# First head's loads issued ahead of the last chunk's third pair of modulation loads, its low keys and biases one step sooner

## The reference, cut to what matters

```python
m_lat = adaln(c, w_mod[l], b_mod[l])                 # silu(c) @ w_mod + b_mod: six vectors of 2048, for c and c_ctx
h = modulate(rms_norm(ys, norm_mix[l]), m_lat[0], m_lat[1])
q, k, v, u = mixer_proj(h, w_in[l])                  # h @ w_in, 2048 x 4096
att = neighbourhood_attention(q, k, v, cache_k[:, l], cache_v[:, l], rpb[l])
mix = jnp.concatenate([att, pool_mixer(u, w_pool[l], pool_scale[l])], axis=-1) @ w_out[l]
ys = ys + m_lat[2][:, None] * mix
...
s_lat = q . k (window of 12 x 32 keys) * scale + bias   # bias from rpb, -1e30 outside the window
s_ctx = q . k_ctx (512 cached keys) * scale
p = softmax(concat(s_lat, s_ctx)); o = p @ (v, v_ctx)
```

## Time and profile before

| | |
|---|---|
| three runs | 3972.54 us (3972.15 to 3976.68) |
| the profiled execution | 3971.88 us, its span 3970.1 us |
| mean granted TensorE clock | 0.975 |
| PE busy over the span | 95% |
| PE / DVE / ACT / POOL busy, 1000 to 1200 us | 183.2 / 117.2 / 101.6 / 95.7 us |
| input projection ends | about 1064.5 us |
| attention | about 1065.7 to 1630 us |

### The profile page before, as it was taken

One profiled execution on the slowest core, in us unless ns is written; L12 is line 12 of the kernel. 1 busy time (PEld: TensorE's weight loads), 2 busy tenths in 40 slices (PEclk: granted clock), 3 DMA queues, 4 the chain that ended last, 5 costly groups with the idle time before them and its releaser, 6 DMA issues. The chain is left out here.

```text
span 3970.1 us, 63525 instructions
## 1 busy us (share of the span) xinstructions
PE 3764.5 (95%) x22936; PEld 3367.7 (85%) x22936; DVE 2455.5 (62%) x4637; ACT 1774.2 (45%) x2654; POOL 472.3 (12%) x517
## 2 busy tenths in 40 slices
PE   8999999999989999999987899999999999999992
PEld 4799999999988888888876788888888888888981
DVE  4745555555566666332225677777777777777774
ACT  3611111111367776311104666666666666665653
POOL 0000000000264644010101000000000000000000
PEclk9999999999999999999998899999999999999996
DMA  9434434433654645645317587888788778888886
GB/s 378 146 129 138 137 124 137 137 130 131 187 168 137 203 144 173 258 144 215 139 40 298 186 259 259 266 264 262 255 275 259 254 261 264 262 263 265 264 251 249
DMA packets 556531, 825.31 MB, mean 208 GB/s; under 512 B 24320, under 2 KB 426144, under 8 KB 544672
## 3 DMA queue, kind: packets, MB, share of 16 engines
q1 hardware_dynamic: 532384, 702.27, 53.4%
q0 software_dynamic: 24064, 121.93, 9.4%
HBM read 717.18 MB, written 108.00 MB: 208 GB/s over the span
## 5 line engine op out<-in xcount | busy, mean ns | idle before, releaser
L2159 DVE TENSOR_TENSOR e_wlo<-e_raw,e_whi 128x1024 fp32r<-128x1024 f32 x768 | 905.2, 1219 | 327.2 <-ACT e_whi L2078 323.9
L2296 PE MATMUL ps<-e_xs,e_whi 128*128 128x320 f32 x4096 | 1054.8, 344 | 10.0 <-DVE e_xs L2173 6.9
L2296 PE MATMUL ps<-e_xs,e_wlo 128*128 128x160 f32 x4096 | 934.9, 238 | 0.0
L2078 ACT ACTIVATE e_whi<-e_raw 128x1024 fp32r<-128x1024 f32 x768 | 766.0, 1049 | 284.8 <-DMA e_raw<-in_w_down 106.4
L2296 PEld LDWEIGHTS ps<-e_xs,e_wlo 128*128 128x128 f32 x4096 | 770.3, 191 | 0.7
L2296 PEld LDWEIGHTS ps<-e_xs,e_whi 128*128 128x128 f32 x4096 | 752.8, 188 | 14.4 <-issue 7.3
L2314 PE MATMUL ps<-e_whi,e_h 128*128 128x512 f32 x1024 | 403.1, 394 | 0.9 <-DVE e_h L2199 0.9
L531 PE MATMUL ps<-hhi,p_whi 128*128 128x428 f32 (+1 forms) x1536 | 381.8, 357 | 8.4 <-DVE p_wlo L463 8.4
L481 DVE SCALAR_TENSOR_TENSOR p_acc<-p_modraw,cT,p_acc 128x256 f32<-128x256 f32 x960 | 386.6, 478 | 0.3 <-DMA p_modraw<-in_w_mod 0.3
L531 PE MATMUL ps<-hlo,p_whi 128*128 128x428 f32 (+1 forms) x1536 | 382.4, 357 | 0.0
L531 PE MATMUL ps<-hhi,p_wlo 128*128 128x428 f32 (+1 forms) x1536 | 380.3, 356 | 0.0
(11 more groups left out here) (252 smaller groups left out, 5359.0 us busy)
## 6 DMA issues: line engine op xcount, KB each, us to landing
e_raw<-in_w_gate SPq DMA_DIRECT2D x64, 2048.0 KB, 7.9
e_raw<-in_w_up SPq DMA_DIRECT2D x64, 2048.0 KB, 7.8
e_raw<-in_w_down SPq DMA_DIRECT2D x64, 2048.0 KB, 8.0
p_modraw<-in_w_mod SPq DMA_DIRECT2D x128, 512.0 KB, 3.5
m_raw<-in_w_mod SPq DMA_DIRECT2D x16, 2048.0 KB, 13.3
p_raw<-in_w_in SPq DMA_DIRECT2D x64, 512.0 KB, 4.7
o_raw<-in_w_out SPq DMA_DIRECT2D x16, 2048.0 KB, 9.0
projT<-p_out_st POOLq DMA_DIRECT2D x30, 640.0 KB, 3.8
```

Source lines behind the costliest of these rows:

```text
L2078: nc.scalar.activation(piece(whi, c, q), piece(raw, c, q), ACT.Copy).then_inc(w_hi_made, 1)
L2159: nc.vector.tensor_tensor(piece(wlo, c, q), piece(raw, c, q), piece(whi, c, q).bitcast(F32), ALU.subtract).then_inc(w_lo_made, 1)
L2296: last = nc.tensor.matmul(bank[:, 0:cols], w[:, s, at:at + P], xs[:, k, 0:cols], start=(k == 0 and w is whi), stop=(k == KD - 1 and w is whi))
```

## The change

SP's loop now covers chunks 0 to 14, and chunk 15 is written out behind it. In chunk 15 `first_loads` comes behind the load of the third w_in quarter, ahead of the two w_mod pieces of that quarter, so ahead of the fourth w_in quarter too; it still waits for the stores of chunk 14 and for one used quarter. POOL makes the low keys once two quarters are used (three before), head 0's biases once three are, head 1's once four are. DVE makes the high keys behind the sums of the third quarter (q = 2) and no longer behind those of the fourth; low queries stay behind those of the fourth. To have the tiles free at these times, `kll` and `q8`, `prT`, `st` and `pscn` change rows, and `pu`, `inv` and `pd` go to a fixed offset in HIGH.

```diff
@@ sync
-            with sp.Fori(0, NCH) as n:
+
+            def load_chunk(n, head_after=None):
                 for q in range(NQ):
                     sp.wait_ge(w_lo_made, n * NQ + (q + 1))
                     sp.dma_start(raw[:, q % RING], quarter(w_in, q, n * CW)).then_inc(w_loaded[q % RING], 16)
+                    if q == head_after:
+                        sp.wait_ge(stored, 2 * LASTC * 16 + FIRST)
+                        sp.wait_ge(piece_used, quarters_used(1))
+                        first_loads()
                     for i in range(2):
                         m, part = q // 2, 2 * (q % 2) + i
                         sp.wait_ge(mod_step, n * (8 * QSTEPS) + (2 * q + i + 1) * QSTEPS)
                         sp.dma_start(modraw[:, i], quarter(w_mod, part, n * (2 * CW) + (MB0 * P + m * CW))
                                      ).then_inc(mod_in[i], 16)
-            sp.wait_ge(stored, 2 * LASTC * 16 + FIRST)
-            sp.wait_ge(piece_used, quarters_used(1))
-            first_loads()
+
+            with sp.Fori(0, LASTC) as n:
+                load_chunk(n)
+            load_chunk(LASTC, 2)
@@ gpsimd
+            pool.wait_ge(piece_used, quarters_used(2))
+            low_keys()
             pool.wait_ge(piece_used, quarters_used(3))
-            low_keys()
-            biases()
+            biases(0)
             pool.wait_ge(piece_used, quarters_used(4))
+            biases(1)
             pool.wait_ge(mod_turned, 2 * NCH + RING)
@@ vector
-                    if q == NQ - 1 and not following:
+                    if q == NQ - 2 and not following:
                         dve.wait_ge(piece_used, quarters_used(2))
                         high_keys()
+                    if q == NQ - 1 and not following:
                         low_queries()
@@ attention
-    mask, kraw, vc, kx, khh, q8, bias, prT, pairs, athi, pllo, st, pscn = row_of(
+    mask, kraw, vc, kx, khh, kll, bias, pairs, athi, pllo = row_of(
         LOW, ...
-    brow, qraw, vT, qst, vL, kll, atlo, plhi, wpn, pu, inv, pd = row_of(
+    brow, qraw, vT, qst, vL, q8, atlo, plhi, wpn, prT, st, pscn = row_of(
         HIGH, ...
+    pu, inv, pd = row_of(HIGH + 59 * 1024, ("pu", [P, PW], F32), ("inv", [P, TOK], F32), ("pd", [P, TOK], F32))
...
-        def biases():
+        def biases(h):
             pool.wait_ge(mask_in, 16)
-            make_bias(0, 0, True)
-            make_bias(0, 1, True)
+            make_bias(0, h, True)
```

More of the change, by code:

```diff
@@ L667, in attention @@
         ("a_mean", [P, 2, TOK], F32), ("pc", [P, 2, PW], F32))
-    mask, kraw, vc, kx, khh, q8, bias, prT, pairs, athi, pllo, st, pscn = row_of(
+    mask, kraw, vc, kx, khh, kll, bias, pairs, athi, pllo = row_of(
         LOW, ("mask", [P, 6, NKL], F32), ("kraw", [P, KCOL], F32), ("vc", [P, PAST // P, P], F32), ("kx", [P, CTX], F32),
-        ("khh", [P, 2, KCOL], F32R), ("q8", [P, TOK], F32),
-        ("bias", [P, 2, 6, NKL], F32),
-        ("prT", [P, 2, 1024], F32), ("a_pairs", [P, W, P], F32), ("athi", [P, TOK], F32R), ("a_pllo", [P, TOK], F32R),
-        ("a_st", [P, 4, 8], F32), ("a_pscn", [P, 1], F32))
-    brow, qraw, vT, qst, vL, kll, atlo, plhi, wpn, pu, inv, pd = row_of(
[L675 to L678, removed]
+        ("khh", [P, 2, KCOL], F32R), ("kll", [P, 2, KCOL], F32R), ("bias", [P, 2, 6, NKL], F32),
+        ("a_pairs", [P, W, P], F32), ("athi", [P, TOK], F32R), ("a_pllo", [P, TOK], F32R))
+    brow, qraw, vT, qst, vL, q8, atlo, plhi, wpn, prT, st, pscn = row_of(
+        HIGH, ("brow", [P, 2, 16 * 48], F32), ("qraw", [P, TOK], F32), ("vT", [P, TOK], F32),
+        ("qst", [P, 2, TOK], F32R), ("vL", [P, 4, KC * ROWS], F32), ("q8", [P, TOK], F32),
+        ("atlo", [P, TOK], F32R), ("a_plhi", [P, TOK], F32R), ("a_wpn", [P, 2, P], F32), ("prT", [P, 2, 1024], F32),
+        ("a_st", [P, 4, 8], F32), ("a_pscn", [P, 1], F32))
+    pu, inv, pd = row_of(HIGH + 59 * 1024, ("pu", [P, PW], F32), ("inv", [P, TOK], F32), ("pd", [P, TOK], F32))
     BATCH_AT = {1: 4, 12: 0, 14: 1, 17: 2, 19: 3}
```

## The result

The changed kernel takes 3979.52 us as the median of 20 runs (3971.47 to 3987.77); the kernel before, in 20 runs on the same chip, 3973.67 us (3964.17 to 3980.6). The medians differ by 5.9 us; the ratio is given as 1.0016 with a 95% interval of 1.0009 to 1.0023, so 6.4 us more with 3.6 to 9.1. That is within the 0.2% of "no change", and in the range of 3966 to 3982, at its slow end. The profiled execution took 3978.77 us, span 3977.0 us, mean granted clock 0.975.

A forecast was written before the change was run, and what follows sets the result against it. TensorE, busy 95% of the span, was taken as the bound. Terms 13.2 - 1.3 + 1.6 - 5.7 - 6.1 = +1.7 us on 3971.88 gave 3973.6, stated as a 3974.0 median; 8-in-10 range 3966 to 3982.

The forecast's parts named there:

- one turn each: Seam before attention: the last quarter's 16 sums alternate with POOL's instructions and end at 1076.0; this forecast had 0.50.
- The queue: SyncE, last chunk: head loads start 23.9 us sooner, w_in quarter 3 lands at 1045.9, costing PE nothing before 1048.2.
- POOL beside the sums: Seam before attention: late sums make PE wait at L540, first transpose at 1078.9 instead of 1065.69, +13.2 us.
- V copy: Start of attention: PE's 1.30 us wait for the V copy on ACT goes, -1.3 us.
- Clock at the start: Start of attention: PE leaves a long wait at low clock, +1.6 us net of the replaced stretch at 1074.
- Second head's wait: Second head: PE's 3.62 us wait for POOL's low keys goes with 2.1 us of clock, -5.7 us.
- The stall at L1104: First pair: PE's 4.18 us stall shrinks to 1.5 us, -2.7, and 3.4 us of clock goes, -6.1 us together.
- a rival: No exclusion for L481: sums end at 1061.8, total 3969.3, down to 3965.5 us; shared full queues might lessen gains; chance 0.13.
- The starved rival: Last sums and L1104: DVE gets no turn while POOL runs on, 3974.0 + 8.0 = 3982.0 us; chance 0.17.
- the 6.76 us row: L1104 beside POOL's run once took 6.76 us, outlasting several instructions; cited as evidence for DVE getting no turn.

The follow-up runs named there:

- version 2: Changed kernel, but POOL holds the first pair's biases until the last modulation sum, high keys staying early; median 3968.75 us, ratio 0.999 to the kernel before.
- 4: Kernel before plus twelve two-input POOL additions beside the sums of quarter 2 in the last chunk; one run, 3974.1 us.
- 3: Changed kernel with the first pair's twelve biases filled by memsets instead of computed; one run, 3964.09 us.
- 5: Kernel before plus 27 POOL memsets starting beside the sums of quarter 2 in the last chunk; one run, 3978.16 us.
- 1: Changed kernel with DVE's high keys back behind the last quarter's sums; median 3966.44 us, ratio 0.9995 to the kernel before.
- version 9: Kernel before with pauses between POOL's bias additions alone, low-key subtractions still end to end; 3955.27 us, ratio 0.9952.
- version 11: Changed kernel with pauses between POOL's bias additions alone; 3960.82 us, ratio 0.9969 to the kernel before.

## Why the prediction was right, and where its terms were off

The verdict, the sign and the range held, and the mechanism that I put first, one turn each between POOL and the sums, is what happened. Two terms were off, by -4.8 and +8.8 us, and it is partly luck that they cancelled as far as they did: with the first alone corrected the sum would have been below the kernel before. Term by term:

**The queue.** Quarter 3 of w_in reached ACT at +36.3, forecast +38.1. It cost PE nothing, as forecast. kx, 10.5 us from issue to landing (11.1 in the earlier trace rows), landed at 1038.5, that is +32.1 where I took +32.7; the three loads of 512 KB behind it then took 4.15 us, 379 GB/s, where I had taken 283 from the earlier trace rows. Two readings were rounded down, 4.26 us to 4.2 and 0.77 to 0.7; neither moves the sum. From the view of DMA issues, 1020 to 1068:

```profile
kx<-projT SPq DMA_DIRECT2D x1, 128.0 KB, 10.5
```

**POOL beside the sums, +13.2.** It measured +8.4; PE waited 7.08 us where I had said 11 to 13. One turn each was right: a median of 1230 ns a sum; versions 2 and 4 show the same price, 3 and 5 that memsets on POOL don't ask it. Too large were the landing and the keys behind it (high keys end at +45.6, not +47.6: 2.0 us), the sums (18.2 us behind the keys, not 20.6: 2.4) and the restart behind them (2.5 us, not 2.9: 0.4), which makes the 4.8. The Trainium skill (SBUF — State Buffer, "Who interferes with whom") has the second instruction to issue blocked for the whole of the first; the stream of sums agrees with it (1.23 us against 0.48 alone), the lone `atlo` of the first pair does not, since it outlasts up to ten of POOL's instructions.

**V copy, -1.3**: right (waits of 2.0 us in this stretch before, 0.7 after). **Clock at the start, +1.6**: low by about one. From the first transpose to the first `Kx` copy PE's stretch is 1.2 us longer in spite of the 1.3 won, so 2.5. The granted clock there, in windows (PEclk is third from the end; against 0.57 over 4 us in the earlier trace rows with 1.00 around it):

```profile
1072.60:1076.00 3.40, 3.29 (x13) 2.99 (x14) 0.63 (x2) 0.60 (x1) 3.10 (x5) 0.50 0.69 152
1076.00:1080.00 4.00, 2.89 (x13) 2.12 (x12) 2.30 (x8) 2.31 (x3) 0.14 (x1) 0.77 1.02 234
1080.00:1084.00 4.00, 2.67 (x9) 2.37 (x10) 0.77 (x2) 2.74 (x6) 0.00 (x0) 0.65 1.01 240
```

**Second head's wait, -5.7**: right in the profile, no wait at 1107.03 and the clock full over what follows:

```profile
1107.00:1111.30 4.30, 4.30 (x34) 4.03 (x34) 2.10 (x8) 3.26 (x7) 2.58 (x2) 1.00 1.04 224
```

But this wait is a difference of two chains and moves by itself: in versions 1, 2 and 9 it is 1.6 us, with no repair of it, and 4.0 in the kernel before with all pauses. In versions 1 and 9 POOL began these low keys at +90.5 and +91.1, as before (+91.6), and PE was the later one (first `Kx` copy at +79.2 and +79.8 against +77.2); in version 2 POOL began at +88.8.

**The stall at L1104, -6.1: this step failed.** I wrote "With POOL ahead the low keys start as soon as DVE's high keys allow". They did not: the window's loads were issued 2.1 us sooner after the chunk's start and landed 1.9 us later (POOL waited 10.61 us where it had waited 6.68), the second lot cost 4.41 us where it had cost 1.22, and POOL began the low keys 5.1 us later than before, at +114.8. In the rows of SP's queue it is seen what they met: the next head's loads wait for the low queries, and so were issued from +66.1 on (+60.6 before), with the eight `w_pool_by_block` loads behind them until +79.0 (+70.1 before), so that POOL's loads at +68.7 fell into the middle of them and no longer behind them. I had written down that these loads share full queues, in a rival and for another term, and did not follow it here. PE's wait rose by 3.1 us, and its clock loss hardly fell (0.58 over the 7.1 us behind it, 0.52 in the earlier trace rows: 0.4 us). So the term is some +2.7 and not -6.1.

The sum by measured terms: 8.4 - 1.3 + 2.5 - 5.7 + 2.7 = 6.6; the `Kx` offsets gave +5.7 after the first pair, the medians +5.9 and the ratio +6.4 (3.6 to 9.1). Such agreement is closer than the scatter of two or three microseconds in single profiles allows one to claim.

**The starved rival** (3982.0, chance 0.17) was half of the truth: the sums did get their turns, but the lone instruction of the first pair got none. I had given one rule to both. Had I kept the two apart, with the 6.76 us row as the rule for a lone instruction, the forecast would have been 1.7 + 6.1 = +7.8.

**What stays open.** Why a stream of sums gets a turn at each POOL instruction and a lone one sometimes does not: of the twelve `atlo` above 0.4 us in the kernel before, ten took 0.88 to 1.66 us, about one turn, and two took 6.76 and 6.31. What decides between a wait of 0.88 and one of 6.3 us at nearly the same arrival (below). Whether the early high keys are worth their place in a kernel with pauses was not settled.

## What to carry to other kernels

Before moving a POOL step beside DVE work, ask whether both read two SBUF tensors: then count on each DVE instruction waiting for one POOL instruction (0.74 to 0.9 us here), and on a single one that arrives on the critical path being kept out, in the worst case, for as long as POOL runs end to end (9.7 us here). Look at the maximum, not the mean, of a short DVE instruction's duration; where it is many times its median, a wait between POOL's instructions is the cheap remedy for it (0.4 to 0.5% here), better than any reordering tried here. It does nothing for a stream of them. A step started sooner ends sooner only if its loads land sooner: follow every load behind a moved step to its landing.

## What the runs showed that I had not expected

- A pause of some 0.1 us between GpSimd instructions lets a lone VectorE instruction in that was otherwise kept out for 4.0 to 9.7 us: the longest of 80 falls to 1.15 us, and the kernel before gets 15 to 19 us faster.
- The lone wait goes by the moment of arrival, repeatably over kernels. `atlo` arriving 2.05 us after POOL's run began took 7.31 and 7.30 us (versions 2 and 5), 1.91 to 1.92 us after it only 0.55 and 0.52 (versions 1 and 4), 5.50 us after it 4.01 and 4.00 (versions 1 and 4), 4.05 us after it 6.27 to 6.31 (the seventh pair, all seven kernels without pauses), but 4.66 us after it only 0.88 to 0.91 (four pairs of each) and 2.99 us after it 1.66. Each long one ended at the border of the last two POOL instructions ahead of a pause, or at the pause: the kernel before at 1126.85, when the fifth of six biases was over, the changed one at 1131.48, behind the sixth. With pauses between biases alone it was let in ahead of the first bias (version 9) or behind it (version 11). That is a pattern of these traces, not an explanation.
- GpSimd memsets of 128x448 beside VectorE sums cost these nothing: 14 in 5.61 us, as with POOL idle. Two multiplications that read one tensor (TENSOR_SCALAR, 128x256) took 1.16 us beside them, 0.61 with POOL idle.
- Behind a wait of only 1.48 us TensorE's granted clock can fall to its lower level, and need not: it was 0.83 over the 20 us from 1201 in the kernel before, in a pair 3.5 us longer than the next, and 1.00 over 20 us around the same wait of 1.48 us in the changed kernel.
